# Opening layer 0 of a two-layer hybrid backbone in two halves of the tokens

## The reference

```python
mod = (silu(cond) @ w_mod + b_mod)          # six sets of 2048: sh1, sc1, g1, sh2, sc2, g2
h = rms(x) * (1 + sc1) + sh1
proj = h @ w_in                              # q, k, v | fourier | ssm x,B,C | ssm z | dt | gmlp u,v | gates
q, k, v, f_in, xbc, z, dt_raw, uv, gate_logits = split(proj)
# A attention(q, k, v)   B Fourier(f_in)   C Mamba-2 scan(conv(xbc), z, dt)   D gMLP(u, v)
x = x + g1 * (merge(A, B, C, D, gates) @ w_out)
x = x + g2 * (relu(h2 @ w_ff1)**2 @ w_ff2)   # h2: a second modulated norm of x
```

## Time and profile before

| | us |
|---|---|
| three runs: lowest, median, highest | 4773.15, 4837.24, 5525.47 |
| the profiled execution, its own time | 4768.78 |
| its slowest core, 1: span from first to last instruction | 4767.3 |
| TensorE busy in that span | 4562.7 (96%) |
| VectorE, ScalarE busy | 2463.3 (52%), 1910.8 (40%) |
| GpSimd busy | 914.6 (19%) |

### The profile page before, as it was taken

The page is one execution under the profiler, slowest core; times in us unless marked ns, Lnnn a source line. Parts: engine busy times, 40 slices in busy tenths (PEclk is TensorE's granted clock), DMA queues, the critical chain, the costliest instruction groups (busy, mean ns, idle before and its releaser), DMA issues.

```text
span 4767.3 us, 90058 instructions; the slowest of 8 cores (4731.1 to 4767.3 us)
## 1 busy us (share of the span) xinstructions
PE 4562.7 (96%) x31548; PEld 2878.4 (60%) x31548; DVE 2463.3 (52%) x5081; ACT 1910.8 (40%) x4031; POOL 914.6 (19%) x1362
## 2 busy tenths in 40 slices
PE   3989898999999999999999998999999999999999
PEld 1445455566655777777755544655666567777776
DVE  4266645565546444444564575555654644444343
ACT  2134523333225444353544453333322453535352
POOL 1122110000101232424112201000010014141404
PEclk9979999999999999999999999999999999999999
DMA  8862755446776797979778446334578459494949
GB/s 192 136 118 65 170 99 99 80 85 128 131 198 122 120 152 121 152 118 154 159 191 150 92 109 124 67 63 79 109 136 196 100 95 148 76 151 74 153 72 128
DMA packets 266571, 585.63 MB, mean 123 GB/s; under 512 B 43792, under 2 KB 137488, under 8 KB 265872
## 3 DMA queue, kind: packets, MB, share of 16 engines
q0 software_dynamic: 171072, 441.53, 57.4%
q1 hardware_dynamic: 95056, 138.34, 9.1%
HBM read 818.05 MB, written 129.76 MB: 199 GB/s over the span
## 4 chain that ended last, share of the span: by engine, by line
PE 89%; DMA 6%; issue 2%; DVE 2%; ACT 1%; POOL 0%; SPq 0%; DVEq 0%; ACTq 0%; POOLq 0%
PE psum L1837 38%; PE psum L692 20%; PE psum L1651 18%; PE psum L1616 5%; DMA arena<-wm 2%; PE psum L1092 1%; DMA mgs<-arena 1%; PE psum L833 1%; PE psum L1074 1%; DMA arena<-wg 1%; PE psum L1133 1%; ACT arena L743 1%; DMA arena<-lc 1%; PE psum L1094 1%; DVE arena L754 1%
## 5 line engine op out<-in xcount | busy, mean ns | idle before, releaser
L1837 PE MATMUL psum<-arena 128*128 128x320 f16 x13216 | 1802.8, 299 | 0.0
L1837 PEld LDWEIGHTS psum<-arena 128*128 128x128 f16 x13216 | 1289.5, 98 | 508.7 <-issue 10.1
L754 DVE TENSOR_TENSOR arena<-arena 128x1024 f16<-128x1024 f16 (+9 forms) x2178 | 1080.6, 519 | 662.6 <-PE psum L1837 334.9
L743 ACT ACTIVATE arena<-arena 128x320 f16<-128x320 f32 (+8 forms) x1687 | 825.3, 508 | 870.1 <-DVE arena L754 528.3
L692 PE MATMUL psum<-arena 128*128 128x512 f16 (+2 forms) x5680 | 1092.0, 352 | 16.7 <-DVE arena L758 8.4
L1651 PE MATMUL psum<-arena 128*128 128x320 f16 x6720 | 1009.3, 300 | 14.7 <-ACT arena L743 6.0
L692 PEld LDWEIGHTS psum<-arena 128*128 128x128 f16 x5680 | 556.1, 99 | 504.1 <-issue 98.8
L754 DVE TENSOR_TENSOR arena<-psum,arena 128x320 f32<-128x320 f32 (+5 forms) x1110 | 539.2, 490 | 617.5 <-PE psum L1651 239.9
L1651 PEld LDWEIGHTS psum<-arena 128*128 128x128 f16 x6720 | 637.5, 98 | 330.9 <-issue 92.4
L743 ACT ACTIVATE arena<-psum,arena 128x320 f32<-128x320 f32 (+3 forms) x904 | 487.1, 554 | 664.7 <-PE psum L1837 531.8
L769 ACT COPY arena<-psum 128x320 f32<-128x320 f32 (+6 forms) x683 | 293.5, 440 | 581.8 <-PE psum L1837 259.4
(11 more groups left out here) (107 smaller groups left out, 1455.5 us busy)
## 6 DMA issues: line engine op xcount, KB each, us to landing
arena<-w POOLq DMA_DIRECT2D x256, 512.0 KB, 7.0
arena<-wm POOLq DMA_DIRECT2D x192, 512.0 KB, 7.4
arena<-wg POOLq DMA_DIRECT2D x128, 512.0 KB, 6.2
y<-arena POOLq DMA_DIRECT2D x256, 160.0 KB, 7.3
xs<-arena POOLq DMA_DIRECT2D x192, 160.0 KB, 8.2
arena<-xin SPq DMA_DIRECT2D x32, 640.0 KB, 23.5
arena<-xs SPq DMA_DIRECT2D x32, 640.0 KB, 14.9
arena<-dftA SPq DMA_DIRECT2D x32, 512.0 KB, 4.4
```

The source lines that it names most:

```text
L743: return e.activation(out=lz(o), in_=lz(i), func=func, scale=scale, **kw)
L754: lambda e: e.tensor_tensor(out=lz(o), in0=lz(a), in1=lz(b), op=op), r=r, w=w, prio=S.p - boost, tag=tag)
L1837: ins = e.matmul(ps.ap()[:, 0:SUBS], lhsT=wv(kc), rhs=rhs(kc), start=first and kc == 0, stop=kc == 7, skip_group_check=True)
```

## The change

x is loaded, normed, scaled and multiplied in two halves of 640 tokens, the products in tiles of 320 columns.

- Rows of x become half rows of 320 KB, `XH[h]`; the second half is issued after scale columns 13 (six rows) and 15 (ten rows) have landed. `wu` and the columns from the fourth on wait for row 12 of the first half.
- The first half's norm is one chain of chunks (0,512) and (512,128); seven banks take `wu` products row by row (now L2128), then one more tile, then 16 tiles of the eight `wx` blocks. `WXA` is gone: four `wx` blocks use the ring and four use `MSLOT`.
- The second half's squares (sums in unused parts of hT), norm and scaling (L2105) follow, then its 24 tiles.
- Modulation set 0 gets new slots, `SSLOT`, which lie on the second half of x.
- The bias is computed by 768 matmuls of 32 columns (now L2181) instead of 192 of 128, since the blocks no longer lie next to each other. Shifts are added in the order (0,640), (640,384), (1024,256), and z tiles run in order of tokens.
- The scheduler's bytes and durations for these transfers and matmuls are other numbers.

```diff
         MSLOT = [152, 156, 184, 188]
+        SSLOT = [50, 54, 58, 62, 84]
...
             if l == 0 and s == 0:
-                wa = A(MSLOT[kc % 4], [2048])
+                wa = A(SSLOT[kc % 5], [2048])
...
+        accn = [(0, 512, acc0), (512, 768, acc1[0]), (768, 1024, acc1[1]), (1024, 1280, acc1[2])]
+        acch = [(640, 768, hT[:, 15, 640:896].bitcast(F32)), (768, 1024, hT[:, 14, 640:1152].bitcast(F32)), (1024, 1280, hT[:, 13, 640:1152].bitcast(F32))]
...
-            for t in (range(NT) if l else (0, 1, 2, 3, 8, 9, 4, 5, 6, 7)):
+            for t in range(NT):
...
-            XI = [A(50 + 5 * r, [T], F32) for r in range(16)]
-            RB = A(130, [T], F32)
+            XH = [[A(95 + 2.5 * r, [640], F32) for r in range(16)], [A(50 + 2.5 * r, [640], F32) for r in range(16)]]
+            RB = A(90, [T], F32)
             WF = A(136, [4, 16, 128])
-            WXA = A(50, [4, 16, 128])
...
-            xl = [load(XI[fc], xin[fc], 128 * T * 4, tag="xld") for fc in range(16)]
+            HX, HW = 640 * 640, 640 * 1024
+            def load_half(h):
+                for fc in range(16):
+                    xl[h].append(load(XH[h][fc], xin[fc][:, 640 * h:640 * h + 640], HX, tag="xld"))
+            load_half(0)
+            load_half(1)
...
-                    d.preds.add(xl[13].id)
+                    d.preds.add(xl[0][12].id)
...
-                        d.preds.add(xl[9].id)
+                        d.preds.add(xl[0][12].id)
+            for k, d in enumerate(xl[1]):
+                d.preds.add(cl[13 if k < 6 else 15].id)
+
+            def rstd_half(h):
+                for fc in range(16):
+                    sq_acc(fc, 640 * h, 640, fc == 0, XV(h, fc))
+                S.p -= 60
+                for t0, n in (((0, 512), (512, 128)), ((640, 384), (1024, 256)))[h]:
+                    ps2 = norm_rstd(t0, n)
+                    cp("act", RB[:, t0:t0 + n], lambda ps2=ps2, n=n: ps2.ap()[:, 0:n], n, [ps2], [RB[:, t0:t0 + n]])
+                S.p += 60
...
+            rstd_half(0)
+            tiles = [(b, t0) for b in range(4) for t0 in (0, 320)][:7]
...
+            tile(wf(3), WF[:, 3], 320, ev_f, "uproj", 3)
             p0 = S.p
+            for i in range(4):
+                wr.append(ring(wx[0, XORD[i]], prio=-20.0 + 4.4 * i + 60.0, tag="xproj"))
+                S.ops[-1].dma = HW
+                S.ops[-1].preds.add(cl[(9, 13, 15, 15)[i]].id)
+            for i in range(4):
+                wa = A(MSLOT[i], [16, 128])
+                load(fl(wa), wx[0, XORD[4 + i]], HW, q="pool", w=[wa], prio=-2.0 + 4.4 * i, tag="xproj")
...
+            for i in range(8):
+                for t0 in (0, 320):
+                    tile(xw[i][0], xw[i][1], t0, ev_x, "xproj", i)
+            S.p = p0 - 5
+            accm[0] = acch
+            rstd_half(1)
+            accm[0] = accn
+            for c in range(16):
+                scaled(c, 1)
             mod_push(0, (0,))
             S.p = -40.0
             mod_step(16)
+            S.p = p0 + 36
+            for b in range(4):
+                for t0 in (640, 960):
+                    tile(wf(b), WF[:, b], t0, ev_f, "uproj", b)
+            for t0 in (640, 960):
+                for i in range(8):
+                    tile(xw[i][0], xw[i][1], t0, ev_x, "xproj", i)
...
                     for kc in range(16):
                         for j in range(4):
-                            ins = e.matmul(ps.ap()[32 * j:32 * j + 32, 0:128].rearrange("p (b n) -> p b n", b=4), lhsT=shh[:, kc, :], rhs=w[:, :, kc, 32 * j:32 * j + 32], start=kc == 0, stop=kc == 15)
+                            for b in range(4):
+                                w = WF[:, b, kc, :] if gi == 0 else xw[4 * gi - 4 + b][0](kc)
+                                ins = e.matmul(ps.ap()[32 * j:32 * j + 32, 32 * b:32 * b + 32], lhsT=shh[:, kc, :], rhs=w[:, 32 * j:32 * j + 32], start=kc == 0 and b == 0, stop=kc == 15, skip_group_check=True)
```

More of the change, by code:

```diff
@@ new lines, in scaled, with tile @@
+            def scaled(c, h):
+                for (t0, t1, g) in (((0, 640, 0),), ((640, 1024, 0), (1024, T, 1)))[h]:
+                    x = XV(h, c)[:, t0:t1]
+                    S.op("dve", tdve(t1 - t0, False, 1, 1), lambda e, c=c, g=g, t0=t0, t1=t1, x=x: e.scalar_tensor_tensor(out=hT[:, c, t0:t1], in0=x, scalar=modT[0][:, g, 16 + c:17 + c], in1=RB[:, t0:t1], op0=ALU.mult, op1=ALU.mult),
+                         r=[x, RB[:, t0:t1], "scl%d" % c], w=[hT[:, c, t0:t1]], prio=S.p)
+            def tile(w, wd, t0, evac, tag, blk):
+                ps = PS("D")
+                mmg(ps, lambda a: a[:, 0:320], w, lambda kc: hT[:, kc, t0:t0 + 320], 16, 320, [wd], lambda kc: [hT[:, kc, t0:t0 + 320]], tag=tag)
+                evac(blk, t0, ps)
+                S.p += 2.2
@@ L2111, in ev_x @@
[L2111 to L2122 removed]
+                scaled(c, 0)
@@ new lines, in first_products @@
+                for (b, t0), ps in zip(tiles, banks):
+                    S.op("pe", tmm(320), lambda e, ps=ps, b=b, c=c, t0=t0: e.matmul(ps.ap()[:, 0:320], lhsT=WF[:, b, c, :], rhs=hT[:, c, t0:t0 + 320], start=c == 0, stop=c == 15),
+                         r=[WF[:, b], hT[:, c, t0:t0 + 320]], w=[ps], tag="uproj")
+                S.p += 1.5
+            for (b, t0), ps in zip(tiles, banks):
+                ev_f(b, t0, ps)
+            wf = lambda b: (lambda kc: WF[:, b, kc, :])
+            tile(wf(3), WF[:, 3], 320, ev_f, "uproj", 3)
```

115 lines of the change are left out of this document (37 added, 78 removed).

## The result

The changed kernel took 4835.35 us in the median of five runs (4801.30 to 5162.70), the kernel before 4837.24 in the median of five. Some runs of both were disturbed; without them the ratio is 1.0079, with a 95% interval of 1.0046 to 1.0111. The change costs some 38 us, where 11 us of gain had been forecast.

The account below looks back on a forecast made before the run. The opening was taken as bound by transfers until about 130 us, then by TensorE. The first 272-column product came 339 - 326 = 13 us earlier, less 2 us for clock: 4768.8 - 11 = 4758 us; range 4720 to 4840.

Parts of the forecast that it names:

- 205 us: Layer 0 opening: DMA for set 0 decides when the bias products start, at 205 us against 233.4 before.
- Products at 50, column 15 at 95, the bias products 28 us long: Opening: first products at 50 us instead of 78.9, last scale column at 95 instead of 128, bias products lasting 28 us.
- The price by refills: Bias products: 174 pairs buffered, the other 594 need 4.9 instruction refills of 5.79 us, with products running meanwhile; 28 us.
- 102.5 + 204 x 0.136 = 130 us: Second half's norm: its small matmuls wait in TensorE's order behind 204 products of 0.136 us, so come at 130 us.
- 22 x 3.1 = 68 us: Modulation set 0: from 138 us sixteen blocks, four wz and two next-set blocks load at 3.1 us each, 68 us.
- 22 tiles, "326 us": After the bias: 22 tiles of 4.2 us from 233 us put the attention projection's first 272-column product at 326 us.
- What is won by 400 us is kept: From the attention projection to the end: the 11 us gained earlier last, as core 2's earlier transposes accompany a shorter span.
- Nothing comes of it: Opening: the second half starves TensorE and pushes set 0, so the 11 us vanish; 4769 us, chance 0.1.
- The starved bias: Bias products: 5.79 us per 121 pairs, nothing overlapped, 48 us instead of 28; 4778 us, slower, chance 0.15.
- The signs that would have shown it wrong: Bias length within 12 or over 39 us; start before 190 or after 220; another standstill over 10 us; no 0.81 stretch.
- The clock as a rival: Experiments' rival for the opening: lower granted TensorE clock takes back whatever repairs win; no chance was given.

Follow-up runs that it names:

- s3_pin: Changed kernel with ScalarE's squares of half 2 behind the evacuations and its norm products behind 160 products, not 204; mean bias start 233.4 us, no ratio.
- s9_three: Changed kernel with casts ahead of the shift additions, wide bias products, and half-2 squares behind evacuations (norm behind 160 products); ratio to the kernel before 0.9997.
- s4_ring: Changed kernel with modulation set 0 loaded through the ring's two free slots instead of five places under half 2 of x; mean bias start 264.0 us, no ratio.
- s5_early: Changed kernel with set 0 loaded earlier, into second halves of the x tiles' places, and wz loads behind its last block; ratio to the kernel before 1.0066.
- s6_best: Changed kernel with all four repairs: early casts, wide bias products, half-2 squares behind evacuations, set 0 in the x tiles' places; ratio to the kernel before 0.9992.
- a0_again: The changed kernel itself, unchanged, timed again on another chip; ratio to the kernel before 1.0083.
- s1b_casts: Changed kernel with only the shift operand's memset and two casts put ahead of the 48 shift additions; ratio to the kernel before 1.0031.
- b1_narrow: The kernel before with its 192 bias products of 128 columns written as 768 of 32, nothing else; ratio to the kernel before 1.0030.
- s7_late: s6_best with half 2's norm behind 208 products instead of 160, and loads of later sets and wz behind set 0; ratio to the kernel before 0.9993.

## Why the prediction was wrong

The forecast was a gain of 11 us, and the change costs some 38. The step that failed is the start of the bias products, "205 us": 28 us earlier than before was forecast, and on the mean of the cores they start 10.7 us later. Three things are missing in it: TensorE's waits for ScalarE ahead of the norm, the places that hold up set 0, and the wait for the casts. The median of 4835 us lies inside the stated range of 4720 to 4840; that is the width of the range and the spread of the runs, and speaks for nothing in the working. Its own steps, on core 1:

- *Products at 50, column 15 at 95, the bias products 28 us long.* Right: 48.45, 94.97 and 26.9 us (251.81 to 278.67). The price by refills was the right one, and so was their number, five for 4.9. That the length came out so close is partly luck: the gaps were shorter (2.2 to 6.2 us, 18.5 in sum, instead of 28), and the products' own 8.4 us did not run inside them, as the forecast had it, but came on top.
- *"102.5 + 204 x 0.136 = 130 us" for the norm.* It came at 148.0. Of the 18 us, 10.2 are the three waits for evacuations, of which the working had nothing: it put products, weights and rows in order, but not ScalarE, which squares the incoming rows in the same order as it empties PSUM. The other 7 are the price: 204 products took 34.7 us net, 0.17 each, at a granted clock of 0.82, not 0.136. s3_pin and s9_three take the waits away and bring the norm 12 us forward.
- *Set 0 as "22 x 3.1 = 68 us".* From its first load (157.5, forecast 138) to its last product it took 80.8 us, and 83.6 to the last of the two blocks of the next set, which the forecast counted in (138 to 205, 67 us). The step counted bandwidth; what held it was a chain of places: 28 us without a load, since a place is freed by a product behind 168 others. s4_ring shows the same chain tighter, s5_early that earlier loads bring 9 us. Once the squares are repaired they bring nothing (s9_three and s6_best), so most of this term is the late norm passed on.
- *Bias start 205.* It was 251.8. The 46.8 us are 18 (norm), 1.5 (scaling), 16.6 (set 0 and the two blocks) and 10.7: the wait for the casts, not in the forecast at all. In a0_again, where no core was at 0.81 there, the bias starts at 240.4 on the mean, so some 11 of the 46.8 go with core 1's clock. The 48 additions ahead of the casts stood in the kernel before as well. Behind it is an unwritten step, that what was hidden stays hidden: four z tiles were its cover, and the prediction took these away without asking what they covered.
- *22 tiles, "326 us" for the first 272-column product.* It came at 361.3 us, 82.6 behind the bias instead of 93: the tiles ran at 0.229 us a matmul, 58.7 us for 256, at the full clock, where the earlier trace rows had 0.263. The 0.81 stretch was not gone but earlier on core 1, in 100 to 200 us by the windows. This error of 10 us is the one in the kernel's favour.
- *What is won by 400 us is kept.* In sign, yes, and more was added. On the mean of the cores the state matmuls are 34.5 us later. With the cores at 0.81 left out, a0_again against the kernel before, they are 36.7 us later: 8.7 bias start, 19.4 bias length, 8.6 behind it. From there to the end of the span it is 4364.4 us in the changed kernel and 4370.1 in a0_again, against 4357.0 before. The versions with early casts have 4354 to 4365 and the one other with late casts, s5_early, 4372. In s1b_casts it is 4355.6, so moving two casts seems to be worth more than their wait. Of the 14.5 us between it and a0_again 11.7 are idle time of TensorE (97.8 and 86.1 us behind the state matmuls, mean of the cores). What it waits for stays open: the modulation blocks account for 2 (11.0 and 9.0 us), and equally many, 28, had been multiplied by the state matmuls in both.

Of the rivals, none named the whole mechanism. "Nothing comes of it" had a part of it: a late norm of half 2 that pushes set 0. The norm was 18 us late, and all that was granted for it was the 11 us. The starved bias had the right sign and 48 us where 26.9 were measured; the two casts and ScalarE were in nobody's list. The signs that would have shown it wrong were the right ones to name: the bias start after 220 us was one of them.

The clock as a rival that takes back whatever is won falls: on the chip of the second round the granted means rise with the repairs, from 0.982 to 0.986 in a0_again to 0.987 to 0.990 in s6_best, and behind the bias the changed kernel's core 1 shows 1.00 (300 to 361 us). Inside the bias stretch TensorE is granted 0.50, the lower level of 1.2 GHz, in the changed order: after a wait of 11 us in a0_again, and after waits of 3 and 6 us in s1b_casts. In b1_narrow, busy up to the start, it is 0.70 in 237 to 250 us and 0.50 in 250 to 264 (core 2). It costs little there: 128 pairs take 1.35 to 1.43 us in all of them, and the stretch is as long in b1_narrow (25.9 us) as in a0_again (26.7).

## What to carry to other kernels

When a change brings the first half of a pipeline forward, list for each engine that serves both halves what stands in order on it: one late operand of the new half (a row to square) blocks the urgent work of the old (emptying PSUM). When cover is taken away (here four z tiles), look up what ran under it and what it ended with; a 12 us block of additions ahead of a 0.5 us cast costs nothing until nothing is left beside it. And price tiny matmuls by pieces: at 11 to 15 ns a pair of load and matmul the instruction stream sets the time, at 137 ns a product it doesn't show, and one wide instruction for four narrow ones is worth 18 to 21 us here. Last, before two versions are compared by their landmarks, leave out the cores that were held at another clock: two of eight in one trace made a step of 5.5 us here that isn't there.

## What the runs showed of the hardware

- 128 pairs of weight load and 32-column matmul run in 1.4 us, and then TensorE stands for 2 to 7 us; the instruction queue moves one packet of 16 KB for each standstill. In the narrow versions 768 pairs took 24.5 to 29.9 us on the mean of the cores, at DMA shares of 0.42 to 0.84. The first standstill and the last are the long ones (5.7 and 5.1 us on core 2 of b1_narrow), those between 2.4 to 3.7. Even 256 pairs of 64 and 128 columns have one of 1.9 to 5.8 us.
- The granted clock of 0.81 comes on a pair or two of cores for some 100 us or more and is not tied to one stretch: core 1 in 340 to 410 us of the kernel before, but in 100 to 200 us of the changed one, and cores 6 and 7 behind the bias in s7_late, whose state matmuls came at 398 and 405 us when the other six had 371 to 383. Where the slowest core of a run is one of these, its rows overstate or understate a step.
